# The end of a mixture-of-experts step: sums moved off GpSimd, early gathers split round a store, two tiles' sums on the array

## The reference, cut to what matters

```python
def _grouped_moe(h, ...):
    ...                                  # two experts and two gates per token
    for e in range(N_EXPERTS):
        he = jax.nn.silu(t @ w_gate[e]) * (t @ w_up[e])
        out = out + gates[:, e:e + 1] * (he @ w_down[e])
    return out

x = x + (g2 * ffn).astype(x.dtype)       # g2: 1024 values per sequence
return _rmsnorm(x, p['final_norm_g'])    # mean of squares, root, times a row
```

## Time and profile before

| | us |
|---|---|
| runs | 850.99, 852.44, 852.96 |
| median | 852.44 |
| the profiled execution: its time | 852.94 |
| its span, first to last instruction | 851.1 |
| outside the span | 1.84 |
| busy in the span: PE, DVE, ACT, POOL | 776.9, 583.8, 479.8, 98.8 |
| mean granted TensorE clock | 0.975 of 2.4 GHz |

### The profile page before, as it was taken

How to read it: one execution, slowest core, us unless ns; L and a number is a source line. 1 busy time by engine, 2 the same in 40 slices (tenths; PEclk the granted TensorE clock), 3 DMA queues, 4 the chain that set the end, 5 groups by cost and what they waited for, 6 DMA issues and landing times.

```text
span 851.1 us, 13548 instructions
## 1 busy us (share of the span) xinstructions
PE 776.9 (91%) x4188; PEld 586.8 (69%) x4189; DVE 583.8 (69%) x729; ACT 479.8 (56%) x540; POOL 98.8 (12%) x158
## 2 busy tenths in 40 slices
PE   2799999999999999599987799999999999999857
PEld 0477777778787878278864577777777787777522
DVE  1375564747465564875568777888888788888586
ACT  5324464545364554672344567877777777777303
POOL 3000202111111202120004600000000000000430
PEclk9989999999999999799999899999999999999989
DMA  8928194957758391910008999857999999997643
GB/s 318 347 104 266 36 348 109 321 129 271 199 202 266 135 341 60 326 55 1 0 2 347 378 367 382 325 210 317 384 391 383 392 390 405 393 408 264 207 144 124
DMA packets 94971, 213.85 MB, mean 251 GB/s; under 512 B 4634, under 2 KB 55898, under 8 KB 88803
## 3 DMA queue, kind: packets, MB, share of 16 engines
q1 hardware_dynamic: 89620, 194.16, 63.0%
q0 software_dynamic: 2880, 10.49, 3.3%
q10 hardware_dynamic: 2448, 8.91, 2.6%
HBM read 181.56 MB, written 44.56 MB: 266 GB/s over the span
## 4 chain that ended last, share of the span: by engine, by line
PE 71%; DMA 13%; DVE 7%; SPq 3%; issue 2%; ACT 2%; POOL 1%; DVEq 0%; POOLq 0%; ACTq 0%
PE z L1180 31%; PE fill_ps L1901 17%; PE z L1901 10%; PE z L1144 5%; DMA exp_w<-in_exp_w_up 3%; DMA ada_w<-in_ada_w 2%; PE fill_ps L1818 2%; DMA ada_w<-in_sb_w_o 2%; DMA exp_w<-in_exp_w_down 2%; PE z L1278 1%; DVE exp_w L1064 1%; DMA slots_in<-h_tok,row_i 1%; SPq L1435 1%; PE fill_ps L1824 1%; DMA exp_w<-in_exp_w_gate 1%
## 5 line engine op out<-in xcount | busy, mean ns | idle before, releaser
L538 DVE TENSOR_TENSOR w_lo<-exp_w,w_hi 128x1024 fp32r<-128x1024 f32 x192 | 223.3, 1216 | 56.5 <-ACT w_hi L534 56.2
L534 ACT ACTIVATE w_hi<-exp_w 128x1024 fp32r (+1 forms) x192 | 196.0, 1054 | 68.5 <-PE z L1180 44.2
L1180 PE MATMUL z<-w_hi,x_slotT_hi 128*128 128x512 f32 x288 | 124.2, 431 | 10.8 <-DVE w_lo L538 8.3
L1180 PE MATMUL z<-w_lo,x_slotT_hi 128*128 128x512 f32 x288 | 115.4, 401 | 0.0
L1180 PE MATMUL z<-w_hi,x_slotT_lo 128*128 128x512 f32 x288 | 92.2, 401 | 0.3 <-DVE x_slotT_lo L965 0.3
L1901 PE MATMUL fill_ps<-h_hi,wp_hi 128*128 128x512 f32 x192 | 78.2, 407 | 1.6 <-DVE h_lo L1669 1.5
L1901 PE MATMUL fill_ps<-h_lo,wp_hi 128*128 128x512 f32 x192 | 77.1, 402 | 0.0
L1901 PE MATMUL fill_ps<-h_hi,wp_lo 128*128 128x512 f32 x192 | 76.5, 398 | 0.0
L1180 PEld LDWEIGHTS z<-w_hi,x_slotT_hi 128*128 128x128 f32 x288 | 55.5, 193 | 28.1 <-DVE w_lo L538 9.7
L1180 PEld LDWEIGHTS z<-w_lo,x_slotT_hi 128*128 128x128 f32 x288 | 55.5, 193 | 15.3 <-issue 3.8
L1180 PEld LDWEIGHTS z<-w_hi,x_slotT_lo 128*128 128x128 f32 x288 | 55.0, 192 | 14.3 <-DVE x_slotT_lo L965 1.1
(11 more groups left out here) (346 smaller groups left out, 1498.5 us busy)
## 6 DMA issues: line engine op xcount, KB each, us to landing
exp_w<-in_exp_w_gate SPq DMA_DIRECT2D x18, 2048.0 KB
exp_w<-in_exp_w_up SPq DMA_DIRECT2D x18, 2048.0 KB
exp_w<-in_exp_w_down SPq DMA_DIRECT2D x17, 2048.0 KB
ada_w<-in_ada_w SPq DMA_DIRECT2D x12, 2048.0 KB, 10.2
slots_in<-zeros SPq DMA_DIRECT2D x7, 2048.0 KB, 12.7
w_pair<-in_sb_w_qkv SPq DMA_DIRECT2D x24, 512.0 KB, 5.5
slots_out<-y_slot ACTq DMA_DIRECT2D x17, 512.0 KB, 10.4
x_slot<-slots_in SPq DMA_DIRECT2D x16, 512.0 KB, 10.1
```

The costliest lines, as they stand in the source:

```text
L534: act.activation(w_hi[:, u % RING, :].unsqueeze(1), raw_unit(b, u), ACT.Copy).then_inc(hi_ready, 1)
L538: dve.tensor_tensor(w_lo[:, u % RING, :].unsqueeze(1), raw_unit(b, u), w_hi[:, u % RING, :].bitcast(F32).unsqueeze(1), ALU.subtract).then_ ...
L1180: return pe.matmul(out, lhsT, rhs, start=start, stop=stop, skip_group_check=True)
```

## The change

GpSimd loses its three additions. It issues two early gathers, waits for the store of slot m, and then issues the other three early and the five late gathers. VectorE does all early additions, in a new order. ScalarE takes the sigmoid of the last slot ahead of the copy of the pick matrix. For places 1 and 2 PE adds `x_tok` and `late_y` separately, each with an identity matmul, and VectorE no longer adds them there. The diff:

```diff
     def phase_b_pool(pool):
-        for t in TILES:
-            pool.indirect_dma_start(out=early_y[:, t, :], ...).then_inc(early_gathered[t], 16)
-        def add_early(i):
-            t = TILES[i]
-            pool.wait_ge(early_step, i + 1)
-            pool.tensor_tensor(x_tok[:, t, :], x_tok[:, t, :], early_y[:, t, :], ALU.add).then_inc(x_added[i], 1)
-        add_early(0)
+        def gather_early(ts):
+            for t in ts:
+                pool.indirect_dma_start(out=early_y[:, t, :], ...).then_inc(early_gathered[t], 16)
+        gather_early(TILES[0:2])
         pool.wait_ge(exp_loaded[2], 16 * (m + 1))
         pool.wait_ge(y_slot_stored, 16 * (m + 2))
+        gather_early(TILES[2:])
         for t in TILES:
             pool.indirect_dma_start(out=late_y[:, t, :], ...).then_inc(gathered[t], 16)
-        for i in range(1, 3):
-            add_early(i)
...
     def phase_b_act(act):
-        act.wait_ge(pick_turned, 1)
-        act.activation(last_pick_T[:, :], turned_pick, ACT.Copy).then_inc(pick_kept, 1)
         act.wait_ge(unit_used, units_before(m + 1) + RING)
         act.wait_ge(hid_ready, m + 2)
         act.activation(sig[:, :], zb(0), ACT.Sigmoid).then_inc(gate_sig, 1)
+        act.wait_ge(pick_turned, 1)
+        act.activation(last_pick_T[:, :], turned_pick, ACT.Copy).then_inc(pick_kept, 1)
...
     def phase_b_dve(dve):
         rest_of_up(m + 1, range(2))
-        for i in range(2):
-            gated_y(early_y, TILES[i], 0, early_step)
-        rest_of_up(m + 1, range(2, 3))
-        gated_y(early_y, TILES[2], 0, early_step)
-        rest_of_up(m + 1, range(3, RING))
+        gated_y(early_y, TILES[0], 0, early_step)
+        rest_of_up(m + 1, range(2, RING))
         gate_by_sig(m + 1)
-        gated_y(early_y, TILES[3], 0, early_step)
+        gated_y(early_y, TILES[1], 0, early_step)
+        add_early(0)
         keep_hid(m + 1)
         keep_hidT(m + 1)
-        gated_y(early_y, TILES[4], 0, early_step)
-        for i in range(3, NT):
+        add_early(1)
+        for i in range(2, NT):
+            gated_y(early_y, TILES[i], 0, early_step)
             add_early(i)
-        for i in range(2):
-            gated_y(late_y, TILES[i], 1, late_step)
-            add_late(i)
-        gated_y(late_y, TILES[2], 1, late_step)
         ...                              # y_last, two halves
-        add_late(2)
+        for i in range(3):
+            gated_y(late_y, TILES[i], 1, late_step)
+            if i == 0:
+                add_late(i)
+        dve.wait_ge(all_but_last[0], 1)
...
         def other_rows(i):
-            pe.wait_ge(all_but_last[i], 1)
-            for c in range(2):
-                cols = slice(512 * c, 512 * c + 512)
-                mm = acc(last_ps(i)[:, cols], ident[:, :], x_tok[:, TILES[i], cols], stop=True)
+            if i < 3:
+                pe.wait_ge(x_added[i], 1)
+                pe.wait_ge(late_step, i + 1)
+            else:
+                pe.wait_ge(all_but_last[i], 1)
+            for src in (x_tok, late_y) if i < 3 else (x_tok,):
+                for c in range(2):
+                    cols = slice(512 * c, 512 * c + 512)
+                    mm = acc(last_ps(i)[:, cols], ident[:, :], src[:, TILES[i], cols], stop=(src is not x_tok or i >= 3))
             mm.then_inc(last_mm, 1)
```

More of the change, by code:

```diff
@@ L606, in phase_b_pool @@
         pool.nop(nofuse=True)
-        for t in TILES:
-            pool.indirect_dma_start(out=early_y[:, t, :], out_offset=None, in_=slots_out[:, :],
-                                    in_offset=bass.IndirectOffsetOnAxis(ap=fetch_i[:, t, 0:1], axis=0)
-                                    ).then_inc(early_gathered[t], 16)
-        def add_early(i):
-            t = TILES[i]
-            pool.wait_ge(early_step, i + 1)
-            pool.tensor_tensor(x_tok[:, t, :], x_tok[:, t, :], early_y[:, t, :], ALU.add).then_inc(x_added[i], 1)
-        add_early(0)
+        def gather_early(ts):
+            for t in ts:
+                pool.indirect_dma_start(out=early_y[:, t, :], out_offset=None, in_=slots_out[:, :],
+                                        in_offset=bass.IndirectOffsetOnAxis(ap=fetch_i[:, t, 0:1], axis=0)
+                                        ).then_inc(early_gathered[t], 16)
+        gather_early(TILES[0:2])
         pool.wait_ge(exp_loaded[2], 16 * (m + 1))
```

## The result

| | before | after |
|---|---|---|
| median of the runs, us | 852.7 | 843.1 |
| lowest and highest of the four runs shown with the result | 850.99, 854.64 | 842.59, 845.35 |
| profiled execution: time, span | 852.94, 851.1 | 843.55, 841.8 |
| mean granted TensorE clock | 0.975 | 0.978 |

The ratio after to before is 0.9892 with a 95% interval of 0.9864 to 0.9920. The changed kernel is 1.1% faster, and the median is the forecast one.

A forecast was written before the change was run, and what follows sets the result against it. Only the tail counts: VectorE stands still while GpSimd adds, and PE waits on it. -10.94 - 2.27 + 3.44 = -9.77; 852.94 - 9.77 + 0.2 = 843.4, as median 842.9, forecast 843.1; range 841.5 to 846.0, 8 in 10.

The forecast's parts named there:

- Low parts and hidden row: In the last slot's tail, PE's 3.25 us wait goes and the hidden row starts 4.82 us earlier, at 805.05.
- The down product "as before": On PE after the hidden row: same durations as before, 7.13 us for the product, ending at 814.86.
- `y_last` held by VectorE, 0.84 after the product: VectorE's early sums end at 815.7, so `y_last` starts 0.84 us after the down product, before 6.96: 6.1 us more gained.
- `y_last` to PE's last stretch: PE's last stretch starts 1.37 us after `y_last` as before, at 817.07, which is 10.94 us earlier.
- Low clock at the head of that stretch, 2.27 us regained: The first six records of PE's last stretch took 4.85 instead of 2.58 us at low clock; 2.27 us taken as gained.
- Four more matmuls, 3.44 us, PE the bound: In PE's last stretch, four more matmuls of two records each add 3.44 us unhidden; VectorE beside it has slack 0.8.
- Store and gathers: Slot m's store lands at 802.2, GpSimd's next gather goes at about 803.0; removed overlap costs 0 to 2.7 us, taken 0.2.
- The third, a lock-out of GpSimd: GpSimd's gathers get no turn while VectorE runs back to back: +7.1 us, 850.2; chance 0.05.
- Rival 1: The tail's records on PE start at 1.2 GHz as before: +2.27 us, 845.4; chance 0.12.
- the sum's 843.4: The profiled execution's time: 852.94 less 9.77 for the tail, plus 0.2 for store and gathers.
- its own working (842.9): The sum of 843.4 put 0.5 lower, as the median of the runs lies below the profiled execution.

The follow-up runs named there:

- adds_for_nothing: The changed kernel with three more GpSimd additions, 128x896 in a spare buffer nobody reads, at the places of the old ones; 847.41 us.
- before_filled: The kernel before with 24 useless 512-column matmuls on PE in its 6.37 us wait for the plain copy of the last slot's rows; 850.54 us.
- pick_first: The changed kernel with ScalarE's copy of the pick matrix ahead of the sigmoid again, as before; 842.93 us.
- y_last_after_late: The changed kernel with `y_last` behind the gated late tiles of places 0 to 2 on VectorE; 850.86 us.
- late_sums_on_dve: The changed kernel with the late sums of places 1 and 2 back on VectorE and four matmuls fewer on PE; 845.91 us.
- five_early_first: The changed kernel with all five early gathers ahead of the wait for the second-last slot's store, as before; 843.89 us.
- pool_sums_back: The changed kernel with GpSimd again adding the early tiles of places 0, 1 and 2, VectorE's order otherwise the new one; 847.05 us.

## Why the prediction was right, point by point

The forecast and the trace, piece by piece, in us:

| piece | before | forecast | after |
|---|---|---|---|
| first low parts to hidden row | 18.39 | 13.57 | 13.54 |
| hidden row to end of the down product | 9.81 | 9.81 | 11.35 |
| down product's end to `y_last` | 6.96 | 0.84 | 0.11 |
| `y_last` to PE's rows of place 1 | 3.24 | 2.23 | 2.54 |
| from there to PE's end | 15.17 | 17.36 | 17.33 |
| PE's end to the end of the span | 6.05 | 6.05 | 6.12 |
| sum | 59.62 | 49.86 | 50.99 |

- **Low parts and hidden row.** Right to 0.03. The stall beside GpSimd's sums is real (adds_for_nothing), and the new order adds to it: the sums moved alone shortened this piece by 2.4 us, the whole change by 4.85.
- **The down product "as before".** This step failed, by 1.54 us. I had taken two idle pieces of about 1 us as harmless because they were so in the one trace I had. In most of the traces since, the clock was at 1.2 GHz for part of the product, that of the kernel before in before_filled among them (8.82). So 7.13 was one of two outcomes of the same program, and the piece got longer between the two traces without the change being shown as its cause. In the kernel before a slow product costs nothing, `y_last` still comes 4.6 us after it; in the changed kernel it is what `y_last` waits for.
- **`y_last` held by VectorE, 0.84 after the product.** The mechanism changed over: PE came last, by 0.75. This is why the error above cost only 0.8 of its 1.54. pick_first, where the clock stayed up, shows the forecast's own case, to 0.1 us.
- **`y_last` to PE's last stretch.** 0.31 more than forecast. I had PE through with the first half of `y_slot` before `y_last`; since ScalarE's first half now waits for the down product too, PE has four records there and not two.
- **Low clock at the head of that stretch, 2.27 us regained.** Right (before_filled). It was part of the 6.4 us wait's price: in y_last_after_late it came back, as 3.1.
- **Four more matmuls, 3.44 us, PE the bound.** Right to 0.03, and no PE wait in `other_rows(1)`. What they stand for is as dear or a little dearer (late_sums_on_dve).
- **Store and gathers.** GpSimd went on at 802.25, in the clock of the trace of before about 802.9, forecast 803.0. VectorE waited for none of them. That I charged 0.2 us was too much by 0.2; that the split buys nothing held (five_early_first).
- **Rivals.** The third, a lock-out of GpSimd, didn't come: of eight gather issues beside a busy VectorE two were stretched, to 1.85 and 1.61 us, and the next one had its turn. The other six took 0.94 at most, so a VectorE instruction under way doesn't always make an issue longer, as I had read from two. Rival 1 came in another place, the down product.
- **The time of the profiled execution.** The tail gave 8.63 us of the 9.39 between the two profiled executions, and 0.67 came from ahead of it. The forecast tail was 9.56 to 9.77. So the tail came out 1.13 us too long (50.99 for 49.86), and the 0.67 from ahead of it, 0.09 outside the span and the 0.2 charged for nothing cover nearly all of that: 843.55 for the sum's 843.4. The forecast of 843.1 itself lies 0.2 above its own working (842.9), with no reason given. That the median fell on it to 0.1 is luck, since single executions scatter by 2 to 7 us.

The Trainium skill, "SBUF — State Buffer", section "SBUF: two separate sides", states the exclusive lock for a VectorE instruction with two SBUF inputs against a GpSimd instruction that reads SBUF. The traces agree: 2.70 and 2.58 instead of 1.28 and 1.22 with two SBUF inputs (adds_for_nothing), 1.27 unchanged with one input in PSUM (pool_sums_back).

## What to carry to other kernels

Before giving GpSimd a helper's share of elementwise work, count what VectorE does beside it: here an addition of 2.4 us on GpSimd replaced one of 1.15, and three of them held VectorE up by 6.5 us in the kernel before, by 4.3 to 5.1 under the new order. Order a busy engine by who waits for each result: two instructions of 0.6 us, placed four instructions later, cost 6.8 us. And price a wait of PE with the slow matmuls behind it, here 1.1 us after a wait of 1.9, and 2.3 to 3.1 after waits of 3.6 to 6.4.

## What the runs showed of the hardware

- A VectorE product with one operand in PSUM ran at 1.27 us in the midst of GpSimd additions that doubled the length of products with both operands in SBUF.
- The granted clock fell to 0.50 in down products that had only two idle pieces of 0.85 to 1.2 us shortly ahead, in seven traces, with 7.13 us becoming 8.6 to 8.8, and in an eighth behind pieces of 1.86 and 1.04, with 10.1 us. Three traces with the same short pieces stayed at 1.00. What tells these apart isn't settled, and the length of the pieces doesn't: 1.02 and 1.19 us stand before 7.13 in one trace and before 8.80 in another.
- The same program's head, up to the last slot, ended 2.7 us apart in two executions, with no edit in it.
- The time of the kernel before goes with the mean granted clock of the execution: a median of 854.8 us at 0.969, of 851.9 at 0.977.
